# Order of the last expert weights, discarded passes at the start and the final norm's row in a one-core decoder block

## The reference, cut to what matters

```python
h = rmsnorm(x, norm_mix); proj = h @ w_in                    # 1024 x 6424
y_a = nsa_attention(...)     # compressed, selected and window branches, T5 bias
y_r = retention(...)         # chunkwise, rotary, group norm, swish gate
merged = sigmoid(gate_a) * (y_a @ w_nsa_up) + sigmoid(gate_r) * (y_r @ w_ret_up)
x = x + merged @ w_out
h = rmsnorm(x, norm_ffn)
# 32 experts; each token goes to 2 of them
x = x + sum over experts e of combine[:, e] * ((silu(h @ w_gate[e]) * (h @ w_up[e])) @ w_down[e])
return rmsnorm(x, norm_final)
```

## Time and profile before

| | us |
|---|---|
| median of 3 runs | 497.41 |
| lowest, highest | 496.32, 501.41 |
| the profiled execution | 497.04 |
| its span, first to last instruction | 495.2 |
| TensorE busy | 464.6 |
| VectorE busy | 210.1 |
| ScalarE busy | 89.4 |
| GpSimd busy | 34.3 |

### The profile page before, as it was taken

The page is one execution under the profiler, slowest core; times in us unless marked ns, Lnnn a source line. Parts: engine busy times, 40 slices in busy tenths (PEclk is TensorE's granted clock), DMA queues, the critical chain, the costliest instruction groups (busy, mean ns, idle before and its releaser), DMA issues.

```text
span 495.2 us, 6356 instructions
## 1 busy us (share of the span) xinstructions
PE 464.6 (94%) x2498; PEld 258.3 (52%) x2498; DVE 210.1 (42%) x499; ACT 89.4 (18%) x243; POOL 34.3 (7%) x58
## 2 busy tenths in 40 slices
PE   5999999999999999999999989999999989879783
PEld 2499745564455545544445846455463626226441
DVE  1563019928766668779422452223121212112013
ACT  1000006314332110100011612111021201002012
POOL 0700060400000011000012100000000000000001
PEclk9999999999999999999999999999999988989998
DMA  8999679317016009879993699999999999999952
GB/s 263 412 377 236 214 270 375 135 42 300 0 46 295 0 21 410 333 292 405 364 422 123 270 385 433 408 429 427 409 430 415 422 429 409 431 414 423 428 239 87
DMA packets 20859, 151.32 MB, mean 306 GB/s; under 512 B 2947, under 2 KB 3396, under 8 KB 14172
## 3 DMA queue, kind: packets, MB, share of 16 engines
q1 hardware_dynamic: 19296, 147.88, 73.6%
q0 software_dynamic: 1296, 2.92, 2.8%
q10 hardware_dynamic: 236, 0.08, 0.1%
HBM read 148.25 MB, written 2.62 MB: 305 GB/s over the span
## 4 chain that ended last, share of the span: by engine, by line
PE 70%; DMA 13%; SPq 11%; DVE 4%; issue 2%; ACT 0%; POOLq 0%; POOL 0%; DVEq 0%; ACTq 0%
PE bank L672 31%; PE bank L697 30%; DMA ring<-in_moe_gate_up 12%; SPq L459 8%; PE bank L1094 3%; PE bank L1127 3%; PE bank L703 2%; SPq L456 2%; DMA ring<-in_dense 1%; DVE ring L1619 0%; DVE nsa L1531 0%; DVE nsa L2006 0%; DVE rt L1531 0%; POOLq L148 0%; PE bank L1137 0%
## 5 line engine op out<-in xcount | busy, mean ns | idle before, releaser
L2006 DVE COPY nsa<-bank 128x512 f32<-128x512 f32 x32 | 22.1, 692 | 94.4 <-PE bank L672 73.5
L697 PE MATMUL bank<-ring,x 128*128 128x512 f32 x128 | 57.3, 594 | 0.0
L672 PE MATMUL bank<-ring,nsa 128*32 128x512 f32 x336 | 44.1, 648 | 11.2 <-DMA ring<-in_moe_gate_up 9.4
L697 PE MATMUL bank<-ring,hT_and_y 128*128 128x512 f32 x96 | 43.4, 597 | 0.0
L672 PEld LDWEIGHTS bank<-cst,nsa 128*128 128x128 f32 x256 | 31.2, 196 | 23.4 <-issue 18.0
L1465 ACT ACTIVATE nsa<-bank 128x512 f32<-128x512 f32 x32 | 19.1, 597 | 126.4 <-PE bank L672 108.2
L697 PEld LDWEIGHTS bank<-ring,x 128*128 128x128 f32 x128 | 23.8, 190 | 27.6 <-issue 27.5
L672 PE MATMUL bank<-cst,nsa 128*128 128x32 f32 x256 | 33.9, 282 | 1.2 <-DVE nsa L2006 1.2
L2016 DVE SCALAR_TENSOR_TENSOR cst<-cst,bank 128x64 f32<-128x64 f32 x32 | 7.1, 222 | 57.9 <-ACT cst L1473 57.9
L1127 PE MATMUL bank<-selection,Tb 128*128 128x128 f32 x256 | 30.2, 276 | 0.3 <-DVE selection L1935 0.3
L1094 PE MATMUL bank<-nsa,selection 128*128 128x512 f32 x64 | 29.6, 605 | 0.0
(11 more groups left out here) (258 smaller groups left out, 670.1 us busy)
## 6 DMA issues: line engine op xcount, KB each, us to landing
ring<-in_moe_gate_up SPq DMA_DIRECT2D x21, 2048.0 KB, 19.4
ring<-in_dense SPq DMA_DIRECT2D x17, 2048.0 KB, 11.9
hT_and_y<-in_moe_gate_up SPq DMA_DIRECT2D x6, 2048.0 KB, 21.5
vr_and_gr<-in_moe_gate_up SPq DMA_DIRECT2D x5, 2048.0 KB, 22.9
nsa<-in_moe_down SPq DMA_DIRECT2D x10, 512.0 KB, 21.0
windows<-in_moe_down SPq DMA_DIRECT2D x8, 512.0 KB, 20.6
qkT<-in_moe_down SPq DMA_DIRECT2D x8, 512.0 KB, 20.3
keys<-in_moe_down SPq DMA_DIRECT2D x7, 512.0 KB, 15.5
```

The source lines that it names most:

```text
L672: return nc.tensor.matmul(o, l, r, start=s, stop=e)
L697: ins = nc.tensor.matmul(o, l[:, k, :], r[:, k, :], start=first and k == 0, stop=last and k == n - 1, skip_group_check=True)
L2006: V.tensor_copy(dst, bank[k][:, src]).then_inc(emptied[k], 1)
```

## The change

- `FIRST` has five parts: the old last one is split into row blocks 4 to 5 and 6 to 7. x's two tiles are issued ahead of the last part, the 64 KB of constants behind the second part. VectorE sums x's squares ahead of weighting the last part.
- TensorE does ten products of ones with ones (128 columns) into the bank of "qr1" before its first real product; the first real pass overwrites the bank.
- GpSimd no longer waits for the weighted x before its memsets.
- The second halves of the down weights get a tenth home, the place of the norms' vector; expert 9's second half is loaded there in the first turn, once the feed-forward norm's last use is over.
- `reload_dw(6)` stops at expert 27, `reload_dw(7)` loads both halves of experts 28 to 31.
- The final norm's vector is loaded as one row of 4 KB by GpSimd, behind the first down product of batch 5, into the home that expert 23's first half has left; in the last batch TensorE spreads it over all partitions with two one-row products (jobs NF0.c, NF1.c), ScalarE copies them out, and VectorE waits for the copies.
- In rounds after the first the down weights use homes 4 to 7.

```diff
-FIRST = (range(0, 1), range(1, 2), range(2, 4), range(4, 8))
+WARM = 10
+FIRST = (range(0, 1), range(1, 2), range(2, 4), range(4, 6), range(6, 8))
...
-GATHER_N, DOWN_C = ["G0.n", "G1.n"], ["O0.c", "O1.c"]
+GATHER_N, DOWN_C, FINAL_C = ["G0.n", "G1.n"], ["O0.c", "O1.c"], ["NF0.c", "NF1.c"]
...
-SEG = dict(first=GATHER_N, body=BATCH_C + GATHER_N + DOWN_C, last=BATCH_C + DOWN_C)
+SEG = dict(first=GATHER_N, body=BATCH_C + GATHER_N + DOWN_C, last=FINAL_C + BATCH_C + DOWN_C)
...
-        DW = [[b[:, 0:D] for b in down_homes] + [nsa[:, 3072:4096]], [b[:, D:2 * D] for b in down_homes]]
+        DW = [[b[:, 0:D] for b in down_homes] + [nsa[:, 3072:4096]], [b[:, D:2 * D] for b in down_homes] + [cst[:, C_ROT:C_ROT + D]]]
+        nf = DW[0][3]
...
             for i, ks in enumerate(FIRST):
+                if i == len(FIRST) - 1:
+                    for t in range(TT):
+                        sp.dma_start(x[:, t, :], a["x"][0, t * P:(t + 1) * P, :]).then_inc(s_x[t], 16)
...
-            for t in range(TT):
-                sp.dma_start(x[:, t, :], a["x"][0, t * P:(t + 1) * P, :]).then_inc(s_x[t], 16)
-            sp.dma_start(cst[:, 0:C_MC], a["packed"][:, 0:C_MC]).then_inc(s_cst, 16)
+                if i == 1:
+                    sp.dma_start(cst[:, 0:C_MC], a["packed"][:, 0:C_MC]).then_inc(s_cst, 16)
...
             first_dw(9, (0,))
+            sp.wait_ge(s_xr, len(PIECES))
+            first_dw(9, (1,))
             sp.wait_ge(s_seed, 4)
             first_dw(5)
-            sp.wait_ge(s_xr, len(PIECES))
-            vec(nf, a["norm_final"], s_nf)
...
-                    for e in range(last, min(last + BE, NE)):
+                    first, end = min(last, (NB - 1) * BE if b == NB - 1 else NE), min(last + BE, (NB - 1) * BE if b < NB - 1 else NE)
+                    for e in range(first, end):
...
             pool.memset(relb[:, :], 1.0).then_inc(s_relone, 1)
-            pool.wait_ge(s_xw, KT)
...
             router_rstd(1)
+            pool.wait_ge(*step_full("body", "O0.c", 0, NB - 3))
+            pool.dma_start(nf[0:1, :], a["norm_final"].rearrange("(a n) -> a n", a=1)).then_inc(s_nf, 16)
...
             o0, o1 = begin("qr0"), begin("qr1")
+            pe.wait_ge(s_ones, 1)
+            for i in range(WARM):
+
+                mm(o1[:, 0:P], ones[:, :], ones[:, :], True, True)
...
+                if seg == "last":
+                    pe.wait_ge(s_nf, 16)
+                    for h in range(2):
+                        o = start(f"NF{h}.c")
+                        end(f"NF{h}.c", mm(o[:, :], ones[0:1, :], nf[0:1, h * 512:(h + 1) * 512], True, True))
...
+                if seg == "last":
+                    for h in range(2):
+                        out_of(f"NF{h}.c", nf[:, h * 512:(h + 1) * 512])
...
-            for i, ks in enumerate(FIRST):
+            def weighted_x(i):
                 dve.wait_ge(s_xT[i], 16)
-                for k in ks:
+                for k in FIRST[i]:
                     tsc(xw[:, k, :], xw[:, k, :], norm_cols[:, k:k + 1], None, ALU.mult, ALU.bypass).then_inc(s_xw, 1)
+            for i in range(len(FIRST) - 1):
+                weighted_x(i)
...
             tsc(st[:, 0:2], st[:, 200:202], 1.0 / D, EPS, ALU.mult, ALU.add).then_inc(s_rs, 1)
+            weighted_x(len(FIRST) - 1)
...
+                else:
+                    for h in range(2):
+                        dve.wait_ge(*step_out(seg, f"NF{h}.c", r, 0))
                 out_of("O1.c", o_sb[:, 1, :])
...
-            dve.wait_ge(s_nf, 16)
```

More of the change, by code:

```diff
@@ L248, in build @@
         nffn = cst[:, C_ROT:C_ROT + D]
-        nf = cst[:, C_ROT:C_ROT + D]
         rtmp = yaT[:, 0:2, :].rearrange("p a t -> p (a t)")
@@ L315, in build @@
         s_gu = [sem(f"gate_up_loaded{i}") for i in range(6)]
-        s_dw = [[sem(f"down_half{h}_loaded{i}") for i in range(n)] for h, n in enumerate((10, 9))]
+        s_dw = [[sem(f"down_half{h}_loaded{i}") for i in range(n)] for h, n in enumerate((10, 10))]
         s_out1 = sem("out1_loaded")
@@ L544, in one_round @@
                     for h in range(2):
-                        load_dw(h, j, j, 0)
+                        load_dw(h, j + BE, j, 0)
                 with sp.Fori(0, NB - 1) as b:
@@ L552, in one_round @@
                         for h in range(2):
-                            load_dw(h, j, j, b * BE + BE)
+                            load_dw(h, j + BE, j, b * BE + BE)
             rounds(sp, one_round)
@@ L1229, in weights @@
                         else:
-                            i, ks = j, (j, j)
-                            gu, dw = loads_before(NGU, j, r) + b + 1, [loads_before(n, j, r) + b + 1 for n in NDW]
+                            i, ks = j, (j + BE, j + BE)
+                            gu, dw = loads_before(NGU, j, r) + b + 1, [loads_before(n, j + BE, r) + b + 1 for n in NDW]
                         ws.append((GU[i], [DW[h][ks[h]].rearrange("p (k n) -> p k n", k=2) for h in range(2)],
```

## The result

The changed kernel takes 495.14 us (median of 14 runs, 493.03 to 497.89), the kernel before 497.76 us (14 runs, 494.84 to 501.41). The ratio is 0.994, 95% interval 0.992 to 0.996: faster by 0.6%. The forecast was 495.3 us. The profiled execution took 495.47 us with a span of 493.8, 1.45 us under the span of before.

What follows compares the result with a forecast made beforehand. TensorE bounds the kernel before 290 us, then SyncE's weight stream; 0.4 us gained at the start plus 1.7 at the end, 2.1 off the profiled 497.04, gives 494.9, and 0.4 more for the median gives 495.3 us, range 492.9 to 498.5.

Steps and rivals of the forecast that it cites:

- The start, 0.4 us: Kernel start: discarded passes raise TensorE's clock early; 0.4 us kept of at most 1.9, limited by the third part's landing.
- The 64 KB ahead: Kernel start: constants queued ahead of the third row block's weights delay them 0.16 us, at the full queue's rate.
- The last gates, 5.0 us earlier than the old order: Last batch: four halves fewer ahead of its gate weights, so they land 5.0 us earlier, the last at 470.2 us.
- The last half: End of the weight stream: the last second half of the down weights lands near 479.9 us.
- TensorE now waits 1.2 us for it: Last batch: TensorE waits 1.2 us for the last down half; second halves begin at 480.45 instead of 482.14 us.
- what is late next is the queue itself: Last batch: once the last gate's wait goes, the DMA queue's last half is late; the end's gain is 1.7 us.
- The norm's row: Final norm: 4 KB load takes under 10 us, in place by 435 us; its two products take 1.7 us of TensorE.
- The clock did fall: Rival, last batch: the 1.2 us wait ahead of the second halves drops the clock, 3.0 us lost, 498.3 us; chance 0.10.
- the small transfer: Rival, start: the 64 KB costs 1.0 us, turning 0.4 us gained into 0.4 lost, 496.1 us; chance 0.11.
- the queue did end earlier: Counters a rival: expert 6's gate is delayed, last half lands at 481.2 us, only 0.9 gained, 496.6 us; chance 0.12.
- the row was in time: Counters a rival: the norm's row lands at 466 us, 6 us are lost, about 501 us; chance 0.02.
- At the start other profiles show more than forecast: Touches a rival: the third part comes at 9 us, up to 1.9 us kept at the start, 493.8 us; chance 0.10.

Runs made afterwards that it cites:

- the old order: The changed kernel with the reload limits of before, so 4 halves instead of 8 follow the last gate; ratio 0.9959 to the kernel before.
- the start alone: The kernel before with only the start's edits (ten discarded passes, five parts, x and constants ahead, GpSimd without its wait); ratio 0.9983.
- the second profile: The changed kernel itself, unaltered, timed and profiled a second time; 494.0 us, ratio 0.9924 to the kernel before.
- the old parts: The changed kernel with the four first parts of before, x and constants behind them, discarded passes kept; 493.89 us in one execution.
- the run without the gate fill: The changed kernel without the discarded passes ahead of gates 1 and 2 of the last batch; 493.63 us, ratio 0.9915 to the kernel before.

## Why the prediction was right, and where it was not

*The start, 0.4 us.* Measured 0.5 (22.17 against 22.65; up to 1.0 in the other profiles of this start), by the step as forecast: at most 1.9 us to win, and the third part's landing lets through the rest. Two terms were off without effect: the discarded passes took 4.6 us, not 5.1, and the passes came to 0.43 us apart only within the first row block (5.45, 6.31, 6.81). The stream followed: expert 6's gate went out 0.7 us earlier. The 64 KB ahead, put at 0.16 us, can't be told from nothing.

*The last gates, 5.0 us earlier than the old order, last at 470.2 (469.8 with the start).* Measured 437.16 + 31.1 = 468.3, 1.5 us earlier than that. The last half, forecast at 479.9, landed at 478.4. The mis-sized term is the length of the stream. From the issue of expert 6's gate to the landing of the last half the profile of before shows 191.4 us; with one half fewer I had to take 190.1. The ten profiles with the bytes of the changed kernel have 188.9 to 189.1, and the start alone, with the bytes of before, has 190.4. So a half is worth 1.3 to 1.5 us, little more than the 1.25 that I gave it, and 1.0 us was in the one profile of before alone. There two halves landed 2.6 us apart (26.0 and 28.6 us behind that issue) and two more 2.7 (162.9 and 165.6), where 1.3 is usual; why is open. I took one execution's stream for the stream. The start gave the other 0.3 us.

*"TensorE now waits 1.2 us for it" and "what is late next is the queue itself".* This step failed. In the two profiles of the changed kernel TensorE waited nowhere behind expert 27's gate. With the clock up it wants the last half at 478.5 (480.33 - 1.8) and the half lands at 478.3: a tie, where the sum had it 1.2 us late. In the first profile the clock fell at the wait for expert 27's gate and TensorE came 1.7 us behind the landing. The two errors had opposite signs: the queue was 1.5 us earlier than the sum had it with the start (478.4 for 479.9), TensorE 1.4 us later (480.1 for 478.7). So the last sums moved by 2.07 us (483.97 to 481.90), as forecast 2.1, and that is luck: in the second profile, without the drop, they moved by 3.6. The span moved by 1.45 only, since from the last sums to the end it took 11.9 us instead of 11.3; the start's edits alone show 12.0 and the old parts 11.2, so this varies whatever the end's edits are; the medians moved by 2.6.

*The norm's row.* In place after 6.9 us (forecast: under 10), 29 us before its products. They cost 1.9 us of TensorE, forecast 1.7. The sum put them where the kernel before has a pause of 1.76 us, so that gate 0 stayed at 460.6 and they cost nothing. After the change there is no pause there, and they stand on the path, as the run with them doubled shows.

*The rivals.* The clock did fall, but not where I put it: not in a wait ahead of the second halves, for there is none, but at the waits for batch 6's gates, as at the earlier trace rows. In the old order the wait for the last gate hid such a drop, as in the run of that name. In the changed kernel it cost 1.5 us in the one of two profiles where it fell there. The other rivals did not come: the small transfer did not eat the start, the queue did end earlier, the row was in time. At the start other profiles show more than forecast, but 1.2 us at the most (expert 6's gate at 288.96), not 1.9.

*Two slips in the sums, without effect.* With the third part at 11.0 us the time would be 496.0 us, not 495.9; with the last half at 481.2 us 0.8 us would be gained, not 0.9.

## What to carry to other kernels

When a reordering removes the last wait, redo the sum for the engine that waited, with every filler in it: products that only keep TensorE busy ahead of late weights (4.1 us here) turn from free into path once the weights are early, and they take up the room in which a clock drop would be hidden. Work that needs none of the last transfer belongs ahead of the wait for it; here that moved the last sum by 0.8 us in the traces, less than the times can tell. And a forecast from one profiled execution inherits its clock drops and the length of its stream; here a drop moved the last sums by 1.5 us and a longer stream the landings by 1.0, against a gain of 2.1 to 3.6.

## What the runs showed of the hardware

One-row products: eight passes of 512 columns with one row in the array, 457.79 to 461.48 us, kept TensorE busy, and at 462.1 the granted clock was 0.50 for 3.4 us, with no pause since 443.01. The other 27 drops between 400 and 480 us in the twelve profiles all lie at a wait of TensorE of 1.96 to 4.27 us: they begin at most 0.8 us before its end and 1.3 us behind it. This one alone has no wait near. With four such passes, in nine profiles, the clock did not fall behind them. That the rows of the array count is likely, not shown: it is one execution.

A clock drop can last long without a pause inside: in the run without the gate fill TensorE was busy for all of 444 to 454 us at 0.50, begun behind a wait of 2.00 us. The same execution has another of 10.2 us from 413.06, behind a wait of 1.96 us, with TensorE busy throughout. In the other profiles the drops at such waits lasted 3.4 or 6.8 us. What made these two longer is open.
